# Delta rule: the queries stay unnormalised, and their squares join the sum of the output norm

## What is computed

```
def l2norm(x):
    return x * lax.rsqrt(jnp.sum(x * x, axis=-1, keepdims=True) + 1e-6)

def gated_deltanet(...):
    qkv = silu(causal_dwconv(qkv, conv_w))
    q, k, v = split(qkv)
    q = l2norm(q) * (GDN_DK ** -0.5)
    k = l2norm(k)
    ...
    o = chunk_gated_delta_rule(q, k, v, g, beta)
    o = rmsnorm_2(o, norm_w) * silu(z)      # rmsnorm_2: o * rsqrt(mean(o*o) + 1e-6) * norm_w
    return o @ w_o
```

## Time and profile before

| what | us |
|---|---|
| median of 3 runs (range) | 2650.03 (2649.62 to 2650.58) |
| the profiled execution: its own time | 2650.27 |
| the profiled execution: its span | 2648.5 |
| PE busy | 2623.4 |
| DVE busy | 1499.0 |
| ACT busy | 1456.2 |
| POOL busy | 849.7 |

### The profile page before, as it was taken

How to read it: one execution, slowest core, us unless ns; L and a number is a source line. 1 busy time by engine, 2 the same in 40 slices (tenths; PEclk the granted TensorE clock), 3 DMA queues, 4 the chain that set the end, 5 groups by cost and what they waited for, 6 DMA issues and landing times.

```text
span 2648.5 us, 45346 instructions
## 1 busy us (share of the span) xinstructions
PE 2623.4 (99%) x16762; PEld 2282.7 (86%) x16762; DVE 1499.0 (57%) x2457; ACT 1456.2 (55%) x2146; POOL 849.7 (32%) x443
## 2 busy tenths in 40 slices
PE   9999999999999999999999999999999999999999
PEld 8888998888888998888889999988888899999887
DVE  5543645546543645546556787355455567873654
ACT  5445665445545655445455845664455558456643
POOL 0007672000017675000008754810100186548100
PEclk9999999999999999999999999999999999999999
DMA  7655446555555446656667742566565586325664
GB/s 225 185 180 180 141 155 190 184 191 183 184 180 174 144 160 193 188 183 192 186 163 182 162 88 79 175 189 187 178 197 187 155 192 159 81 81 182 188 187 143
DMA packets 351973, 447.17 MB, mean 169 GB/s; under 512 B 32446, under 2 KB 241344, under 8 KB 351776
## 3 DMA queue, kind: packets, MB, share of 16 engines
q1 hardware_dynamic: 350032, 442.80, 56.7%
q10 hardware_dynamic: 816, 1.21, 0.1%
q0 software_dynamic: 928, 0.45, 0.1%
HBM read 443.31 MB, written 1.05 MB: 168 GB/s over the span
## 4 chain that ended last, share of the span: by engine, by line
PE 94%; ACT 4%; DVE 2%; issue 1%; DMA 0%; SPq 0%; DVEq 0%; ACTq 0%
PE PS L522 29%; PE PS L524 28%; PE PS L523 28%; PE PS L725 1%; ACT wh L547 1%; PE PS L1109 1%; PE PS L1182 1%; PE PS L1172 1%; PE PS L691 1%; PE PS L1049 1%; PE PS L913 1%; PE PS L960 0%; DVE PS L2299 0%; ACT xh L1319 0%; PE PS L826 0%
## 5 line engine op out<-in xcount | busy, mean ns | idle before, releaser
L547 ACT ACTIVATE wh<-ring 128x1024 fp32r<-128x1024 f32 (+2 forms) x840 | 883.7, 1054 | 875.0 <-PE PS L522 867.7
L555 POOL TENSOR_TENSOR wl<-ring,wh 128x1024 fp32r<-128x1024 f32 (+2 forms) x332 | 785.7, 2382 | 1603.7 <-ACT wh L547 1603.2
L555 DVE TENSOR_TENSOR wl<-ring,wh 128x1024 fp32r<-128x1024 f32 x508 | 621.7, 1226 | 612.1 <-ACT wh L547 612.0
L522 PE MATMUL PS<-wh,xh 128*128 128x512 f32 (+2 forms) x1760 | 692.3, 393 | 1.3 <-DVE xl L1921 1.1
L524 PE MATMUL PS<-wh,xl 128*128 128x512 f32 (+2 forms) x1760 | 682.5, 388 | 0.0
L523 PE MATMUL PS<-wl,xh 128*128 128x512 f32 (+2 forms) x1760 | 681.3, 387 | 0.0
L522 PE MATMUL PS<-xh,wh 128*128 128x256 f32 x1536 | 447.9, 292 | 0.1
L524 PE MATMUL PS<-xh,wl 128*128 128x256 f32 x1536 | 434.3, 283 | 0.0
L523 PE MATMUL PS<-xl,wh 128*128 128x256 f32 x1536 | 434.2, 283 | 0.0
L522 PEld LDWEIGHTS PS<-wh,xh 128*128 128x128 f32 x1760 | 330.7, 188 | 68.9 <-issue 3.9
L524 PEld LDWEIGHTS PS<-wh,xl 128*128 128x128 f32 x1760 | 330.4, 188 | 68.5
(11 more groups left out here) (318 smaller groups left out, 2468.5 us busy)
## 6 DMA issues: line engine op xcount, KB each, us to landing
ring<-in_ffn_w_in_dram SPq DMA_DIRECT2D x352, 256.0 KB, 3.0
ring<-in_mix_w_in_dram SPq DMA_DIRECT2D x256, 256.0 KB, 3.7
ring<-in_ffn_w_gate_dram SPq DMA_DIRECT2D x176, 256.0 KB, 2.8
ring<-in_ffn_w_up_dram SPq DMA_DIRECT2D x176, 256.0 KB, 3.0
ring<-in_ffn_w_down_dram SPq DMA_DIRECT2D x176, 256.0 KB, 2.8
ring<-in_w_in_dram SPq DMA_DIRECT2D x176, 256.0 KB, 2.9
ring<-in_ffn_w_out_dram SPq DMA_DIRECT2D x176, 256.0 KB, 2.8
ring<-in_w_branch_dram SPq DMA_DIRECT2D x32, 256.0 KB, 2.9
```

Of the source, the lines that this page charges most:

```text
L522: first_ = mm(o, w[0], x[0], start=start, stop=False, skip_group_check=True)
L547: act_(dst, src, ACT.Copy).then_inc(hi_ready, 1)
L555: (engine or v_).tensor_tensor(dst, src, part_views(t, wh)[0], ALU.subtract).then_inc(lo[t.slot()], 1)
```

## The change

- The queries are not divided by their norm. Their squares, their four sums on PE, their four roots on ACT and their four multiplications on DVE go from the groups QKV1 to QKV3; so do two pairs of table loads. The keys keep theirs. The wait for `btok` moves from j = 0 to j = 4.
- Within the delta rule ACT squares the queries of a group in place once they have been used, with a scale of 128 * sqrt(1e-6) (`qsq`), between the copy of the state and the copy of the first chunk's output.
- Behind `1.vn` DVE adds these squares to the squares of the output (`oq0` to `oq3`), each behind its `osq`. The products `os` on PE wait for `oq` instead of `osq`.
- The epsilon of the output norm's Ln becomes 128 * 1e-12.

```
--- before.py
+++ after.py
@@ -1042,7 +1042,7 @@
 
                 n = j // 2
                 pe.wait_ge(m2[1].sem, m2[1].at(f"l2sq{n}"))
-                if j == 0:
+                if j == 4:
                     pe.wait_ge(m2[1].sem, m2[1].at("btok"))
                 else:
                     pe.wait_ge(m2[2].sem, m2[2].at(f"l2n{j - 1}"))
@@ -1062,7 +1062,8 @@
             group("QKV1", 0)
             for n in range(2, 6):
                 pe.wait_ge(m2[1].sem, m2[1].at(f"cp.QKV{n - 2}"))
-                group(f"QKV{n}", (n + 1) % 2 * 2, {0: lambda: sums(2 * n - 4), 1: lambda: sums(2 * n - 3)})
+                group(f"QKV{n}", (n + 1) % 2 * 2,
+                      {0: lambda: sums(2 * n - 4), 1: lambda: sums(2 * n - 3)} if n >= 4 else ())
             pe_delta(pe, t)
 
             def ready_a(c):
@@ -1230,7 +1231,7 @@
             wa("1.oc.1")
             wv("1.vn")
             for i in range(4):
-                wa(f"osq{i}")
+                wv(f"oq{i}")
                 did(mm(bank(NORM_BANKS[i]), ones, sqp(i), start=True, stop=True), f"os{i}")
             fill()
             fill()
@@ -1612,8 +1613,6 @@
                 act_(z, z, ACT.Silu).then_inc(m2[1].sem, m2[1].did(f"silu{n}"))
 
             def square(n):
-                if n >= 2:
-                    e.wait_ge(m2[0].sem, m2[0].at(f"l2s{2 * n - 3}"))
                 e.wait_ge(m2[1].sem, m2[1].at(f"silu{n}"))
                 act_(sq[:, n % 2 * 4:n % 2 * 4 + 4, :], heads[:, 4 * n:4 * n + 4, :], ACT.Square).then_inc(
                     m2[1].sem, m2[1].did(f"l2sq{n}"))
@@ -1623,11 +1622,7 @@
                 e.wait_ge(m2[0].sem, m2[0].at(f"l2s{j}"))
                 act_(bank(4), bank(4), ACT.Ln, bias=consts[:, 0:1]).then_inc(m2[1].sem, m2[1].did(f"l2.{j}.ln"))
                 e.wait_ge(m2[1].sem, m2[1].at(f"l2.{j}.ln"))
-                if j < 4:
-                    ins = act_(bank(4), bank(4), ACT.Exp, scale=-0.5, bias=consts[:, 3:4])
-                else:
-                    ins = act_(bank(4), bank(4), ACT.Exp, scale=-0.5)
-                ins.then_inc(m2[1].sem, m2[1].did(f"l2.{j}.rstd"))
+                act_(bank(4), bank(4), ACT.Exp, scale=-0.5).then_inc(m2[1].sem, m2[1].did(f"l2.{j}.rstd"))
 
             def gated(num):
                 e.wait_ge(m2[0].sem, m2[0].at(f"p.GLU_G{num}"))
@@ -1657,18 +1652,18 @@
             tables(SILU_TANH)
             for n in range(6):
                 high(e, t, 1)
-                if n >= 2:
+                if n >= 4:
                     tables(LN_EXP)
                     root(2 * n - 4)
                 high(e, t, 1)
-                if n >= 2:
+                if n >= 4:
                     root(2 * n - 3)
                 high(e, t, 1)
-                if n >= 2:
+                if n >= 4:
                     tables(SILU_TANH)
                 if n:
                     silu(n - 1)
-                    if n <= 4:
+                    if n in (3, 4):
                         square(n - 1)
                 high(e, t, 1)
                 e.wait_ge(m2[0].sem, m2[0].at(f"p.QKV{n}"))
@@ -1762,6 +1757,9 @@
                     act_(bank(6, 0, S), bank(6, 0, S), ACT.Copy, scale=1.0 / D).then_inc(cv[1].sem, cv[1].did("mean"))
                 wp(f"{g}.s")
                 copy(st, 3, f"{g}.sc")
+                wv(f"{g}.qd")
+                q_ = heads[:, 4 * g:4 * g + 4, :]
+                act_(q_, q_, ACT.Square, scale=P * EPS ** 0.5).then_inc(dl[1].sem, dl[1].did(f"{g}.qsq"))
                 wp(f"{g}.o.0")
                 copy(oT2[:, 4 * g:4 * g + 4, 0:P], 2, f"{g}.oc.0")
                 if g == 1:
@@ -1780,7 +1778,7 @@
             def root(i):
                 e.wait_ge(dl[0].sem, dl[0].at(f"os{i}"))
                 z = bank(NORM_BANKS[i])
-                act_(z, z, ACT.Ln, bias=consts[:, 0:1], scale=1.0 / P).then_inc(dl[1].sem, dl[1].did(f"o{i}.ln"))
+                act_(z, z, ACT.Ln, bias=consts[:, 3:4], scale=1.0 / P).then_inc(dl[1].sem, dl[1].did(f"o{i}.ln"))
                 e.wait_ge(dl[1].sem, dl[1].at(f"o{i}.ln"))
                 act_(z, z, ACT.Exp, scale=-0.5).then_inc(dl[1].sem, dl[1].did(f"o{i}.rstd"))
 
@@ -2223,7 +2221,7 @@
             ins.then_inc(pro_dve.sem, pro_dve.did("invf"))
             v_.memset(consts[:, 0:1], EPS)
             v_.memset(consts[:, 2:3], math.log(0.5))
-            v_.memset(consts[:, 3:4], -0.5 * math.log(P))
+            v_.memset(consts[:, 3:4], P * EPS * EPS)
             v_.memset(consts[:, 1:2], LN_EPS).then_inc(pro_dve.sem, pro_dve.did("consts"))
             e.wait_ge(x_in[0], 16)
             e.sem_inc(x_upd, 2)
@@ -2368,13 +2366,15 @@
             step(e, m2, v_.tensor_tensor(bgtok, bgtok, btok, ALU.mult), "bgtok")
             for n in range(6):
                 short(n, (0,))
-                if 1 <= n <= 4:
+                if 3 <= n <= 4:
                     unit(2 * n - 2)
                 short(n, (2,))
-                if 1 <= n <= 4:
+                if 3 <= n <= 4:
                     taps(2)
                     unit(2 * n - 1)
                     taps(3)
+                elif 1 <= n <= 2:
+                    taps(5)
                 elif n == 0:
                     taps(5)
             dve_delta(e, taps)
@@ -2515,6 +2515,9 @@
                 wp(f"{g}.ws")
                 wa(f"{g}.uc.1")
                 did(tt(DU["u", 1], DU["u", 1], four(4), ALU.subtract), f"{g}.vn")
+            for i in range(4):
+                e.wait_ge(dl[1].sem, dl[1].at(f"osq{i}"))
+                did(tt(sqp(i), sqp(i), blk2(heads, i), ALU.add), f"oq{i}")
             for i in (0, 2):
                 e.wait_ge(cv[1].sem, cv[1].at(f"ln.sq{i + 1}"))
                 v_.tensor_tensor(lnsq[i], lnsq[i], lnsq[i + 1], ALU.add).then_inc(cv[2].sem, cv[2].did(f"sq.{i}"))
```

## The result

The changed kernel takes 2656.71 us (median of 10 runs, 2656.27 to 2658.59) against 2650.01 for the kernel before; the ratio is 1.0025, with a 95% interval of 1.0018 to 1.0033. It is slower by 6.7 us. The profiled execution took 2656.27, its span is 2654.5, 6.0 more than before.

What follows compares the result with a forecast made beforehand. PE, busy 2623.4 of 2648.5 us, bounds the kernel. Per layer 5.25 - 0.34 = 4.91 lost against 3.44 gained; both layers 9.8 - 6.9 = +2.9, so 2653.1 us (+0.1%), range 2647.5 to 2658.5.

Steps and rivals of the forecast that it cites:

- the likeliest case: Whole kernel: holes of about 5 us in both layers with the clock kept, 2653.1 us; chance 0.50.
- the first rival: PE's hole at the delta rule's end: granted clock falls, 2.35 us more per layer, 2657.8; chance 0.33.
- bound of 0.2%: Whole kernel: times from 2644.7 to 2655.3 count as same; faster 0.04, same 0.65, slower 0.31.
- Sums (-6.9): PE in the QKV groups: eight of 16 sums go, 0.86 us each, all of it counting.
- What goes from ACT and DVE, and the squares on ACT (0): QKV groups: removed work hides behind PE; delta rule: added squares fit ACT's idle time; both 0.
- The queue behind DVE's additions: Delta rule's end: sq.all stands behind four additions, so PE waits 5.25 us per layer for it.
- The meeting with POOL: Delta rule's end: POOL's low part gets in ahead of sq.2, making the hole 5.25 instead of 3.04 us.
- no meeting: Rival, delta rule's end: POOL's low part comes earlier or later, holes of 3.04 us, 2648.5; chance 0.10.
- Given back (-0.34 per layer): Behind the hole: ACT's high part and table load fall into it, so PE's 0.57 wait for cp.Z1 shrinks by 0.34.
- The clock (0 in the likeliest case): PE's hole of 5.1 us: clock taken as kept, the one observed fall being 4.7 us after PE stopped.
- the clock case: Clock falls in one or both layers' holes, mostly 2654.5 to 2660 us; chance 0.33.

Runs made afterwards that it cites:

- no_adds: Changed kernel without the squares of the queries and their additions, os waiting for osq as before: 2643.34 us, ratio 0.9973.
- before_with_adds: Kernel before, all query sums and norms kept, plus the change's squares, additions and wait in the delta rule: 2663.91 us, ratio 1.0052.
- adds_last: Changed kernel with DVE's four additions behind the layer norm's three (sq.0, sq.2, sq.all) instead of ahead of them: 2643.24 us, ratio 0.9975.
- pool_later: Changed kernel with ACT's table load ahead of its high part instead of behind it, so POOL asks later: 2650.75 us, ratio 1.0002.
- hole_filled: Changed kernel with 20 products of ones (128 columns, results unused) on PE between the fill and the wait for sq.all: 2653.14 us, ratio 1.0011.
- adds_last_early_table: Changed kernel with DVE's four additions behind sq.all and ACT's Ln/Exp table load ahead of its wait for 1.o.1: 2642.63 us, ratio 0.9971.
- hole_half_filled: Changed kernel with 10 products of ones (128 columns, results unused) on PE between the fill and the wait for sq.all: 2654.57 us, ratio 1.0016.
- adds_before_last_sum: Changed kernel with sq.0 and sq.2 ahead of DVE's four additions and only sq.all behind them: 2646.03 us, ratio 0.9985.

## Why the prediction was right and where it was wrong

The measured 2656.7 lies in the range, but not at the likeliest case: it is the first rival, the clock that falls in the hole (estimated at 2657.8), which had 0.33. By the prediction's own bound of 0.2% (2655.3) the change is slower, which had 0.31, and not the same, which had 0.65.

- **Sums (-6.9).** Right: 7.1 by `no_adds`, 7.2 by `before_with_adds`.
- **What goes from ACT and DVE, and the squares on ACT (0).** Right: `no_adds` and `adds_last` take the same time. ACT's idle time ahead of `1.oc.1` shrank from 2.03 to 1.50 and covered the square.
- **The queue behind DVE's additions.** Right, and the term that decides: forecast hole 5.25, measured 5.10. The additions come at the forecast pace, 2.50 for four. Most of the difference is PE's start, 0.05 us after the end of `sq.all` (1650.44 + 0.69 = 1651.13 to 1651.18) and not the 0.15 that was taken from another kind of matmul.
- **The meeting with POOL.** Right in place, order and size: `sq.2` ended 0.54 after POOL (0.55 in the earlier trace rows); 5.25 - 3.04 = 2.21 forecast, 2.14 measured by `pool_later`. POOL asked during `sq.0` and got its turn ahead of `sq.2`; in `pool_later` DVE's `sq.all` was running and POOL waited. Both readings agree with the rule that the Trainium skill states in SBUF — State Buffer, "Who interferes with whom": a DVE instruction with two SBUF inputs contends with a GpSimd instruction that reads SBUF, and the order of issue decides who blocks. The case "no meeting" was priced at 2648.5; with the clock held it measures 2648.9.
- **Given back (-0.34 per layer).** Right: `hole_filled` has 0.5 left of 1.1, and `adds_last_early_table` gets the same 0.34 without a hole.
- **The likeliest case as a whole (2653.1)** is `hole_filled`, the changed kernel with the clock held: 2653.14. The agreement in the last tenth is luck: the prediction's own terms add up to 2653.0 (2650.03 + 2.9), and the hole came out 0.15 shorter and the start behind it 0.1 longer.
- **The clock (0 in the likeliest case) is the step that failed.** I had one observation, a fall 4.7 us after PE's last matmul, and took it for the point from which it decides, so that a hole of 5.1 was a close call. Counted in the same way, from the end of PE's last matmul to the fall, the runs show 2.8 us in layer 0 of the changed kernel (1646.24 to 1649.02) and 4.5 in layer 1 (2375.00 to 2379.48), 2.2 and 3.8 in `before_with_adds`, 3.3 and 4.1 in `pool_later`, where PE waited only 2.80, and 3.1 in the one layer of `hole_half_filled`. What I had put down against the rival, that the moment may depend on where the stop falls, is what happened, and it speaks for the rival: the one observation was a late value of a wide spread and not a threshold. With that reading the clock case should have been the forecast. Its price, 4.7 in all, was set from the same 4.7 us and came out 3.6 (2.30 and 1.44 in the trace). Half speed lasted 6.8 us in one layer and 3.4 in the other, but part of that passed while PE still waited.

## What to carry to other kernels

An addition that is small and off the bound engine can cost more than it saves by its place in an in-order stream: before inserting work that waits for something late, list what is queued behind it and who waits for that; here, a few lines further down, the same work costs nothing. Where PE has to wait for some 3 us, add the clock to the price of the hole, or put matmuls whose result isn't used into it (that gave back 3.6 us for two holes of 5.1 and 1.85 for two of 3.0). An operation of DVE with two SBUF inputs on the critical chain should be placed against POOL's operations by their start times. A single observation of when something happens is not yet a threshold.

## What the runs showed of the hardware

- The granted clock fell in all six holes of 2.80 or 4.95 us of waiting that were left empty (changed kernel, `before_with_adds`, `pool_later`, two layers each), in one of two with 2.71 (`hole_half_filled`), and in neither of the two with 1.48 (`adds_before_last_sum`), in the profiled executions. The fall came 2.2 to 4.5 us after the end of PE's last matmul, even where PE was busy again by then (`pool_later`: fall at 1649.32, PE busy from 1648.88). The clock stayed at half for 3.4 us in some holes and for 6.8 in others, also under the same program (6.8 and 3.4 in the two layers of the changed kernel).
- Whether it falls at about 2.7 us of waiting is chance: the same instructions, one layer yes, the other no, and a spread of 3.7 us between runs against 0.9 with PE kept busy.
- The lower clock costs half of the time that PE works under it, and not half of the time that it lasts. In the changed kernel PE worked from 1651.18 to 1655.84 and from 2379.95 to 2382.88 at half clock; half of that is 2.33 and 1.47, and 2.30 and 1.44 were lost, of 6.8 and 3.4 us at half.
- `sq.0` and `sq.2`, DVE additions with two SBUF inputs, took 1.29 us together with POOL out of the way and 3.43 where POOL's low part got its turn between them.
